# A two-layer diffusion backbone: routing rebuilt around raw rows, lists of extra blocks moved into the expert loop, earlier loads of the first experts

## The reference, cut to what matters

```python
h2x = modulate(rmsnorm(xs, norm_ffn_w[i]), sh2x, sc2x)     # x * r(token) * gain(feature) * (1 + scale) + shift
scores = jax.nn.sigmoid(h2x @ router_w)                    # (512, 64)
sel = scores + router_bias
group_scores = top_k(sel.reshape(T, 8, 8), 2)[0].sum(-1)   # the 4 best of 8 groups stay
idx = top_k(where(emask, sel, -inf), 6)[1]
w = scores[idx] / sum * 2.5
# tokens grouped by expert in blocks of 128 rows; an expert with more than 128 tokens has extra blocks
yb = (silu(xb @ exp_w1[e]) * (xb @ exp_w3[e])) @ exp_w2[e]
out = sum over a token's 6 rows of w * yb + the same of a shared expert on all tokens
```

## Time and profile before

| | |
|---|---|
| Time, three runs | 2120.74, 2124.32 (median), 2128.97 us |
| Profiled execution | 2121.22 us, its span 2119.4 us |
| Busy | TensorE 87% of the span, VectorE 41%, ScalarE 22%, GpSimd 18% |
| Granted TensorE clock | 0.95 of full speed over the span |
| DMA | 625 MB, 295 GB/s in the mean, 390 to 410 GB/s in the expert loops |
| Layer 0's experts | first unit starts at 508.7 us, last at 1083.6 |
| Layer 1's experts | first unit starts at 1447.9 us, last at 2019.5 |
| Big units | 10 of 64 in layer 0, 13 of 64 in layer 1; one extra block in each |

### The profile page before, as it was taken

One profiled execution on the slowest core, in us unless ns is written; L12 is line 12 of the kernel. 1 busy time (PEld: TensorE's weight loads), 2 busy tenths in 40 slices (PEclk: granted clock), 3 DMA queues, 4 the chain that ended last, 5 costly groups with the idle time before them and its releaser, 6 DMA issues.

```text
span 2119.4 us, 30756 instructions
## 1 busy us (share of the span) xinstructions
PE 1847.9 (87%) x9520; PEld 983.2 (46%) x9521; DVE 864.2 (41%) x1525; ACT 458.9 (22%) x823; POOL 389.3 (18%) x577
## 2 busy tenths in 40 slices
PE   5999999886998889887999998877888899988996
PEld 3455555434544444444444443344444444544543
DVE  1556767566322222222116499575222212222226
ACT  4144444221111011111011554330111111111112
POOL 0010000011111111111105388012111111111113
PEclk9999999997999999999999999898999999999998
DMA  9488011357999999999988102257999999999955
GB/s 402 182 335 339 1 40 48 151 218 269 397 410 402 398 394 393 404 399 394 373 357 307 76 1 119 86 243 280 391 405 403 399 395 406 390 406 392 395 185 209
DMA packets 95681, 625.11 MB, mean 295 GB/s; under 512 B 16128, under 2 KB 16256, under 8 KB 57472
## 3 DMA queue, kind: packets, MB, share of 16 engines
q1 hardware_dynamic: 44640, 499.70, 58.7%
q0 software_dynamic: 26112, 79.72, 10.4%
q10 hardware_dynamic: 24864, 44.84, 5.8%
HBM read 563.38 MB, written 76.28 MB: 302 GB/s over the span
## 4 chain that ended last, share of the span: by engine, by line
PE 56%; DMA 26%; DVE 8%; POOL 5%; issue 3%; ACT 2%; SPq 0%; POOLq 0%; ACTq 0%; DVEq 0%
DMA ring<-in 23%; PE PS L1171 10%; PE PS L1165 9%; PE PS L1178 5%; PE PS L1192 4%; PE PS L1203 4%; PE PS L1392 3%; POOL work L649 3%; PE PS L1129 3%; PE PS L1082 3%; PE PS L1053 2%; PE PS L1120 2%; PE PS L1015 2%; PE PS L1092 2%; POOL work L617 2%
## 5 line engine op out<-in xcount | busy, mean ns | idle before, releaser
L1171 PE MATMUL PS<-ring,work 128*64 128x256 f32 x3360 | 420.1, 406 | 112.9 <-DMA ring<-in 91.9
L1171 PEld LDWEIGHTS PS<-ring,work 128*64 128x64 f32 x3360 | 260.7, 146 | 248.4 <-DMA ring<-in 97.8
L1581 DVE TENSOR_TENSOR work<-work,PS 64x256 f32<-64x256 f32 x105 | 44.4, 423 | 524.9 <-ACT work L716 523.0
L1178 PE MATMUL PS<-ring,work 128*64 128x512 f32 x840 | 203.3, 605 | 1.3 <-DVE work L1593 1.2
L1165 PE MATMUL PS<-ring,work 128*128 128x512 f32 x400 | 184.1, 615 | 22.4 <-DMA ring<-in 16.1
L569 POOL COPY col_i<-idx 128x1 int32 (+1 forms) x128 | 23.4, 182 | 799.9 <-PE PS L1203 792.4
L1587 DVE COPY work<-PS 128x1024 f32<-128x1024 f32 x128 | 156.8, 1225 | 16.7 <-PE PS L1203 12.8
L575 POOL DMA_INDIRECT work<-h_rows,col_i x128 | 125.1, 978 | 166.0 <-issue 166.0
L1203 PE MATMUL PS<-cst,work 128*128 128x128 f32 x1040 | 142.4, 281 | 14.0 <-DMA work<-h_rows,col_i 14.0
L716 ACT ACTIVATE work<-PS 64x256 f32<-64x256 f32 x105 | 39.5, 376 | 517.9 <-PE PS L1171 515.6
L1203 PEld LDWEIGHTS PS<-cst,work 128*128 128x128 f32 x1040 | 115.0, 142 | 67.1 <-issue 52.4
(11 more groups left out here) (264 smaller groups left out, 2200.7 us busy)
## 6 DMA issues: line engine op xcount, KB each, us to landing
ring<-in SPq DMA_DIRECT2D x156, 2048.0 KB, 8.6
ring<-in SPq DMA_DIRECT2D x132, 1024.0 KB, 10.8
y_rows<-sq POOLq DMA_DIRECT2D x2, 14336.0 KB, 59.5
y_rows<-work ACTq DMA_DIRECT2D x210, 128.0 KB
ring<-in SPq DMA_DIRECT2D x3, 4096.0 KB, 15.4
y_rows<-work ACTq DMA_DIRECT2D x46, 256.0 KB
ring<-in SPq DMA_DIRECT2D x2, 3072.0 KB, 17.2
work<-in SPq DMA_DIRECT2D x2, 2048.0 KB, 17.0
```

The lines of the kernel that those rows point to most:

```text
L1171: last = mm(bank(6)[64 * q:64 * q + 64, 0:F], lhs(c)[:, 0:64], w13(s)[:, q, c, :], start=(c == 0), stop=(c == DC - 1), tile_position=(0, 6 ...
L1178: last = mm(bank(4)[64 * q:64 * q + 64, :], actT[par][:, kk, 0:64], w2(s)[:, kk, q * 512:(q + 1) * 512], start=(kk == 0), stop=(kk == 1), ...
```

## The change

- **Scores in token layout.** The shift term is formed for all 128 partitions (stationary operand the shift, broadcast; moving one the router weights). TensorE turns the standard deviations (one transpose into bank 6) and the raw logits; VectorE takes reciprocals into `r_col` (128x4, a column for each tile of 128 tokens) and forms r * logit + shift in four instructions; ScalarE's sigmoid gives the scores.
- **Raw rows.** TensorE turns `xT`, not `hM`; ScalarE's copy out of PSUM scales each row with its r. Gain and shift are applied in each unit, when the turned rows leave PSUM: eight instructions of 128x128 in place of one of 128x1024 (`rows_scaled`), in the extra blocks too.
- **The normed `hM`** is now needed by the shared expert alone: VectorE's eight products (`norm_rows`) and ScalarE's eight scalings (`scale_shift`) stand two by two behind units 7 to 10; the spread of r (`spread_rows`) behind unit 6 on TensorE. GpSimd's part is gone.
- **Lists of extra blocks.** Counts, row numbers, lists and weights, so far ahead of unit 0 and in units 0 to 2, stand behind units 1 to 6. Eleven units are written out one by one (`HEAD`), then follows the loop.
- **First gathers.** Those of units 0 and 1 read the index list directly, always 128 rows, with no copy, register load or branch.
- **Loads.** In layer 0 experts 0 and 1 are loaded between modulation units during the output projection, experts 2 and 3 at its end; modulation units 8 to 13 lie in `work` and wait for the end of attention. In layer 1 experts 2 and 3 are loaded once the first projection of the convolution is done, 0 and 1 at the end of the last projection; modulation units 15 to 19 wait for the end of the convolution and alternate between two homes (three before).

```diff
@@ unit_home
             if u < LATE:
                 n = 1 + (u - EARLY) % 2
-                return n, n, (u - EARLY) // 2 + 1 + (EARLY // 2 if n == 1 else 0)
-            n = (u - LATE) % 3
+                return n if u < WO_UNITS else 2 + n, n, (u - EARLY) // 2 + 1 + (EARLY // 2 if n == 1 else 0)
+            n = (u - LATE) % 2
+            return (0, 5)[n], n, (u - LATE) // 2 + 1 + (EARLY // 2, LATE // 2)[n]
+        HEAD = 11
+        FIRST_ROWS = HEAD - DC // 2
@@ sync, layer 0
             sp.wait_ge(pj_ps, 6 * NPAIR)
             sp.dma_start(ring[:, 0:DC * D], wo).then_inc(mixer_out_in, 16)
+            sp.wait_ge(o_ps, NPAIR)
+            load_unit(WO_UNITS)
+            load_unit(WO_UNITS + 1)
+            sp.wait_ge(modt_used, WO_UNITS)
+            load_first(0, 0)
+            load_unit(WO_UNITS + 2)
+            load_first(0, 1)
+            load_router(0)
+            for u in range(WO_UNITS + 3, LATE):
                 load_unit(u)
-            sp.wait_ge(o_ps, NPAIR)
-            load_router(0)
-            sp.wait_ge(modt_used, LATE)
+            sp.wait_ge(wo_ps, DC)
+            load_first(0, 2)
+            load_first(0, 3)
             load_moe(0)
@@ sync, layer 1
             sp.wait_ge(glu_ps, DC)
-            for u in range(LATE, UNITS):
+            load_unit(LATE)
+            load_first(1, 2)
+            load_first(1, 3)
+            sp.wait_ge(cv_rdy, DC)
+            for u in range(LATE + 1, UNITS):
                 load_unit(u)
             sp.wait_ge(pw2_ps, DC)
+            load_first(1, 0)
             sp.wait_ge(modt_used, UNITS)
+            load_first(1, 1)
@@ gpsimd
-                norm_half(i)
-                gather(0, 0, xg_in[0])
-                gather(1, 1, xg_in[1])
+                for u in range(2):
+                    pool.indirect_dma_start(out=xg[u], out_offset=None, in_=h_rows[i],
+                                            in_offset=bass.IndirectOffsetOnAxis(ap=idx[:, u:u + 1], axis=0), ...
@@ scalar
+                a.wait_ge(z_rdy, i + 1)
+                A(score, score, ACT.Sigmoid).then_inc(score_rdy, 1)
-                    A(acc[:, t, :], bank(1 if t % 2 == 0 else 4, 2), ACT.Copy).then_inc(hrow_sb, 1)
+                    A(acc[:, t, :], bank(1 if t % 2 == 0 else 4, 2), ACT.Copy, scale=r_col[:, t:t + 1]).then_inc(hrow_sb, 1)
+                for u in range(2, HEAD):
+                    either(u, lambda big: silu(u, 1, u % 2, big))
+                    either(u - 1, lambda big: store(u - 1, 32 * ((u - 1) // 2), (u - 1) % 2, big))
+                    if u >= FIRST_ROWS:
+                        for c in range(2 * (u - FIRST_ROWS), 2 * (u - FIRST_ROWS) + 2):
+                            scale_shift((J_FFN0, J_FFN1)[i], c)
@@ tensor
-                    last = mm(bank(5)[0:E, 0:1], rw_sb[:, c, :], mod[i][:, 3, c, 0:1], start=(c == 0), stop=(c == DC - 1))
+                    last = mm(bank(5)[:, 0:E], mod[i][:, 3, c, 0:1].to_broadcast([128, 128]), rw_sb[:, c, :],
+                              start=(c == 0), stop=(c == DC - 1))
+            def router_scores(i):
+                j = (J_FFN0, J_FFN1)[i]
+                router_shift(i)
+                logits(i, range(DC - 1))
+                mean(j, DC - 1)
+                logits(i, range(DC - 1, DC))
+                pe.wait_ge(std_rdy, norm_turn(j))
+                tr(bank(6)[:, 0:128], rs[:, 0:128], ident).then_inc(std_ps, 1)
+                pe.wait_ge(scoreT_rdy, i + 1)
+                for jj in range(2):
+                    last = tr(bank(7)..., scoreT[:, jj * 128:(jj + 1) * 128], ident)
+                last.then_inc(score_ps, 1)
-                        last = tr(..., hM[:, c, t * 128:(t + 1) * 128], ident)
+                        last = tr(..., xT[:, c, t * 128:(t + 1) * 128], ident)
-                pe.wait_ge(nrm_out, 8 * (J_FFN0, J_FFN1)[i] + DC)
-                for t in range(2):
+                for t in range(TT):
                     rows_of(t)
+                for u in range(HEAD):
+                    unit(u, slot_of(u), slot_of(u - 1) if u else None, 32 * loads_of(u), 16 * ((u + 1) // 2 + 1), u % 2)
+                    if u == 2:
+                        count_before()
+                    elif u == 3:
+                        count_units()
+                    elif u == 6:
+                        spread_rows(i)
+                        extra_slots()
@@ vector
+            def router_z(i):
+                dve.wait_ge(logit_ps, 2 * i + 1)
+                link(V.tensor_copy(shift_row[:, :], bank(5)[:, 0:E]))
+                dve.wait_ge(logit_ps, 2 * i + 2)
+                V.tensor_copy(scoreT, bank(4)[:, 0:T // 2]).then_inc(scoreT_rdy, 1)
+                dve.wait_ge(std_ps, i + 1)
+                V.reciprocal(r_col[:, :], bank(6)[:, 0:128:32]).then_inc(rs_rdy, 1)
+                dve.wait_ge(rs_rdy, norm_turn((J_FFN0, J_FFN1)[i]))
+                dve.wait_ge(score_ps, i + 1)
+                for t in range(TT):
+                    last = V.scalar_tensor_tensor(score[:, t * E:(t + 1) * E], bank(7)[:, t * E:(t + 1) * E], r_col[:, t:t + 1],
+                                                  shift_row[:, :], ALU.mult, ALU.add)
+                last.then_inc(z_rdy, 1)
-                    V.tensor_copy(xgT[par].rearrange("p c t -> p (c t)"), bank(1, 2)).then_inc(xgT_ev, 1)
+                    rows_scaled(par).then_inc(xgT_ev, 1)
+                def rows_scaled(par):
+                    for c in range(DC):
+                        last = V.tensor_scalar(xgT[par][:, c, :], bank(1, 2)[:, c * 128:(c + 1) * 128], modA[i][:, 1, c, 0:1],
+                                               mod[i][:, 3, c, 0:1], ALU.mult, ALU.add)
+                    return last
+                def norm_rows(c0, c1):
+                    src, dst = JOBS[(J_FFN0, J_FFN1)[i]][0:2]
+                    dve.wait_ge(bc_rdy, norm_turn((J_FFN0, J_FFN1)[i]))
+                    for c in range(c0, c1):
+                        V.tensor_tensor(dst(c), src(c), bank(3), ALU.mult).then_inc(nrm_mul, 1)
+                for u in range(HEAD):
+                    either(u, lambda big: product(u, u >= 2, u % 2, big))
+                    rows_out(u + 1, u >= 1, (u + 1) % 2)
+                    act_out(u, u >= 2, u % 2)
+                    if u == 1:
+                        extra_counts()
+                    elif u == 2:
+                        extra_passed()
+                    elif u == 3:
+                        extra_units()
+                        extra_rows()
+                    elif u == 4:
+                        extra_lists()
+                    elif u == 5:
+                        extra_at()
+                    elif u == 6:
+                        extra_idx()
+                        weights()
+                    if u >= FIRST_ROWS:
+                        norm_rows(2 * (u - FIRST_ROWS), 2 * (u - FIRST_ROWS) + 2)
```

More of the change, by code:

```diff
@@ L443, in expert @@
                     expert_down(e, s, done)
[L445 to L450, removed]
                 def refill_up(u, s):
@@ L942, in mod_chunk, with mean @@
                 last.then_inc(modrow_ps, 1)
-            def mean(j, c, between=lambda: None):
+            def mean(j, c):
                 w = JOBS[j][2]
@@ L953, in mean @@
                 last.then_inc(sq_used, 1)
-                if c == DC - 1:
-                    between()
+                if c == DC - 1 and j not in (J_FFN0, J_FFN1):
                     pe.wait_ge(rs_rdy, norm_turn(j))
@@ L1246, in moe @@
                 last.then_inc(pos_ps, 1)
-                for t in range(2, TT):
-                    rows_of(t)
                 for kk in range(K):
@@ L1288, in unit @@
                     turn_act(u, par)
-                unit(0, slot_of(0), None, 32, 16, 0)
-                unit(1, slot_of(1), slot_of(0), 32, 32, 1)
-                pe.wait_ge(xat_rdy, i + 1)
-                for n in range(NK):
-                    last = mm(bank(0)[:, 448:448 + XMAX], at_pos[:, n, :], unit_lo[:, n, :], start=(n == 0), stop=(n == NK - 1),
-                              skip_group_check=True)
-                    if n % TT:
-                        last = mm(bank(0)[:, 448:448 + XMAX], at_pos[:, n, :], unit_hi[:, n, :], start=False, stop=(n == NK - 1),
-                                  skip_group_check=True)
@@ L1299, in moe, with extra_slots @@
-                last.then_inc(xidx_ps, 1)
-                unit(2, slot_of(2), slot_of(1), 32, 32, 0)
-                with nc.tensor.Fori(0, (E - 4) // 4) as g:
+                def extra_slots():
+                    pe.wait_ge(xat_rdy, i + 1)
+                    for n in range(NK):
+                        last = mm(bank(0)[:, 448:448 + XMAX], at_pos[:, n, :], unit_lo[:, n, :], start=(n == 0), stop=(n == NK - 1),
+                                  skip_group_check=True)
+                        if n % TT:
+                            last = mm(bank(0)[:, 448:448 + XMAX], at_pos[:, n, :], unit_hi[:, n, :], start=False, stop=(n == NK - 1),
```

(11 more changed lines are left out.)

197 lines of the change are left out of this document (79 added, 118 removed).

## The result

The changed kernel takes 2145.5 us in the median of four runs (2143.21 to 2148.9), the kernel before 2122.7 beside it (four runs, the three of the table among them): a ratio of 1.0115, 95% interval 1.0096 to 1.0133. It is slower by 1.1%, where 2126 and "no change" were forecast; the time lies at the upper edge of the range, on rival 2's 2145.

What follows compares the result with a forecast made beforehand. It took the expert loops as narrowly DMA-bound, with the DMA idle until unit 0 starts. Unit 0 -14.4, loops +14 and extra blocks +3 gave +2.6 on 2124.3, 2127, stated as 2126 us; range 2106 to 2147.

Steps and rivals of the forecast that it cites:

- rival 2: Expert loops: TensorE's wait for the copy makes its cycle the bound, units 8.6 and 12.0 us; 2145 us, chance 0.25.
- Indices 4.7 us earlier per layer: Routing: GpSimd's products gone (3.2 us) and selection starting 1.6 us earlier bring indices 4.7 us forward, -9.4 in all.
- Indices to transposes 5.0 us: First gather: from index instruction to unit 0's transposes 5.0 us, down from 10.2 and 7.8; together -8.0.
- early prefetch: Expert loads ahead of unit 0: gives little itself, except for the collision with the gather, counted in the gather's gain.
- Row copy of unit 0 +1.5 each: Ahead of unit 0's up-projection: the longer row copy adds 1.5 us in each layer, +3.0.
- Unit 0 14.4 us earlier in all: Start of the expert loops: unit 0 starts 8.4 and 6.0 us earlier in the two layers, -14.4 together.
- modulation loads: Modulation units waiting for attention or convolution: costed at nothing, at most +3 if one is a transfer late.
- Copies 2.72 us: Each unit: eight 128x128 copies out of PSUM take 2.72 us instead of 1.23, bounds 1.77 and 3.3.
- rival 1: Each unit's copies: column operands hidden in a row, eight copies 1.77 us, cycle 7.4; 2110 us, chance 0.28.
- TensorE's pick-up behind the copies: Each unit, from the copies' end to the next up-projection: 0.85 us, making a small unit's cycle 8.3 us.
- Loops +14 (at most +24): Both expert loops together: longer where weights do not set the pace, +14 us, bounds +9 and +24.
- lists of extra blocks: Units 1 to 6: moved list work fits VectorE's 4.6 us free per unit, except 6.2 us of row numbers.

Runs made afterwards that it cites:

- Experiment 6: Changed kernel with copies shared by VectorE and ScalarE, wait behind flag load and branch, plus unread matmuls in TensorE's idle stretches: 28 and 16, 2104.6 us; 20 and 11, 2099.5 us.
- experiment 5: Changed kernel, wait moved, layer 0's experts 0 and 1 loaded late: 2123.0 us; with copies also shared, early loads, first two gathers in old form: 2111.9 us.
- experiment 3: TensorE's wait for the rows moved behind flag load and branch: changed kernel 2114.8 us; kernel before with eight copies 2130.5 us; kernel before 2116.7 us.
- second kernel of experiment 1: Changed kernel with one plain 128x1024 copy per unit in layer 1 alone, gain and shift of its routed inputs left out: 2124.5 us.

## Why the prediction was wrong

- **Indices 4.7 us earlier per layer.** 3.6 and 3.9 (26.5 and 26.4 us behind the mean, where 30.1 and 30.3 stood). The products of selection are at 0.22 to 0.43 us as foreseen. Missing is TensorE's clock: with the row transposes moved away the counting matmuls run at 0.50, a term the sum did not have. Experiment 6 gives it back, and then it is 24.1 us, against 24.4 foreseen.
- **Indices to transposes 5.0 us.** 4.63 and 4.43. Right in size (gains of 5.6 and 3.3, where 5.2 and 2.8 stood). The term held two causes undivided, and its lower bound had the shorter gather path at 1.5 a layer; by itself that gives 1.0. In layer 0 most of the term is early prefetch, of which the prediction says that it "gives little" beyond it: without the early loads the same stretch takes 12.1 us in layer 0, and unit 0 is 6.4 later (experiment 5).
- **Row copy of unit 0 +1.5 each.** From transposes to up-projection it is 5.97 instead of 4.54 us, and 5.73 instead of 4.31: right.
- **Unit 0 14.4 us earlier in all.** From the two means it is 7.7 + 5.8 = 13.5. The modulation loads, costed at nothing, cost nothing: from the first matmul to the last mean of layer 0 it is 0.6 us less than before.
- **Copies 2.72 us.** 2.64. The column operands are not hidden, so rival 1 (1.77) falls. The estimates from two figures of the Trainium skill lie low here: by VectorE: DVE Perf Modes, section on the TRN2 errata, it was 2.07 us, and by Vector Engine (DVE) Microarchitecture Reference, section on measured stream behaviour, 1.7.
- **The step that failed: TensorE's pick-up behind the copies, taken as 0.85 us.** It is 1.14 to 1.40 (1.28 in the unit shown), so the cycle is 8.65 us and not 8.3, a big one 11.9 and not 11.7. I took the 0.7 to 0.8 us of the earlier trace rows, where the wait was long over when TensorE came to it, and gave the cases where TensorE had really waited (1.30 and 0.93) too little weight. The wait stands ahead of the flag load and the branch, so that these hide in one case and not in the other; experiment 3 shows it: with the wait behind them 0.04 us is left.
- **Loops +14 (at most +24).** +37.3. Two mistakes stand in it. The first is the step above. Four tenths of a microsecond weigh much here, because the loops answer to TensorE's cycle only above some length: in every kernel with a small cycle of 7.1 to 7.6 us the loops of the same units take 569 to 580 us (the weights' own pace), and at 8.65 they take 588 to 595. No kernel has a cycle between, so where the price begins is not shown. By TensorE's cycle alone layer 1's loop is 50 x 8.6 + 13 x 11.9 = 585 us. The other 8 stand in unit 0 (10.8 us), and in units 1 and 4 to 7 (10.1, 10.1, 10.3, 9.3, 9.2).
- The second mistake is in those units. The prediction let the lists of extra blocks fit in VectorE's free time, but for the row numbers. They do not, and not only because of the long copies: in layer 1 of the second kernel of experiment 1, with the one copy of before, units 4 to 6 still take 9.95, 10.0 and 9.3 us. Part of it is again the clock: the up-projections of units 0, 1 and 5 of layer 1 begin behind 3.2 to 3.8 us of idle time and take 5.4 to 6.0 us where the others take 3.67.
- **Extra blocks +1.5 each.** The interval from the last unit to the block is 18.96 us instead of 17.68, and 18.98 instead of 17.57: right.
- Rival 2 (pick-up 1.15, cycles 8.6 and 12.0, layer 1's loop 590, 2145 us) is what happened, in its mechanism and its point of decision. That its total agrees to the microsecond is partly luck: its loops are 32 us longer (14 and 18), not 37.3 (16.1 and 21.2). It kept the DMA's hold on the middle of layer 0, where weights now end the wait of only one small and one big unit; and the stretches outside routing and loops, where it had +3, gave -1.8.

## What to carry to other kernels

When an engine's wait ends a cycle, look at what its queue holds between the wait and the work: a register load and a branch behind the wait cost 1.1 to 1.4 us in every iteration in which the engine really waited; ahead of it they left 0.04. Read the pick-up time from places where the engine did wait; where the wait was already over, the same instructions seem free. A loop that is bound by its transfers by a narrow margin hides a longer cycle up to that margin and no further: a copy made 1.4 us longer cost 41 us in 128 units, and 14 once that order was mended with the short copy and with the long one.

## What was not expected of the hardware

TensorE's granted clock falls to 0.50 in stretches where it only waits (0.50 over the counting, behind 4.6 us of waiting), so work moved off it can slow what stays: the counting matmuls went from 3.0 to 5.0 us though they are the same. The loop shows it too. Three units of layer 0 (19, 27 and 43) take 10.4 us instead of 8.7, each with an up-projection like this one, and the window over its first part:

```profile
757.65 5.36 PE L1187 MATMUL PS<-ring,work 128*64 128x256 f32 x32 [1.86 <-issue]
```

```profile
757.60:760.00 2.40, 2.35 (x16) 2.04 (x18) 0.00 (x0) 0.00 (x0) 0.00 (x0) 0.73 0.97 409
```

In this part of the loop TensorE waits 1.6 to 1.9 us ahead of every up-projection; these three stand behind the longest of these waits (1.86), but so do others that run at full clock, and why it falls in these, no run here tells.

The other surprise is that loads which land in time can still cost: the 3.1 MB of expert 0 issued 62 us later and those of expert 1 46 us later (and the other two experts' some 5) held a store of the token rows and the gather behind it for 7 us in all. Yet the weights were not late: the DMA share falls to 0.10 from 500 us on, and the first up-projection, at 505.9, waits for the rows' copy.
